# A macaron transformer step on one core: the opening with the first norm deferred for three panels, tile by tile

## The reference

```python
def modulation(cond, w_mod, b_mod):
    m = jax.nn.silu(cond) @ w_mod + b_mod
    return m.reshape(cond.shape[0], 1, N_MOD, D_MODEL)
def modulate(x, g, shift, scale):
    return rms_norm(x, g) * (1.0 + scale) + shift
def swiglu(h, w_in, w_out):
    g, u = jnp.split(h @ w_in, 2, axis=-1)
    return (jax.nn.silu(g) * u) @ w_out
...
    x = x + m[2] * (0.5 * swiglu(modulate(x, norm_g[0], m[0], m[1]), w_in[0], w_out[0]))
    out, aux = mixer(modulate(x, norm_g[1], m[3], m[4]))
    x = x + m[5] * out
    x = x + m[8] * (0.5 * swiglu(modulate(x, norm_g[2], m[6], m[7]), w_in[1], w_out[1]))
```

## Time and profile before

| | us |
|---|---|
| median of 3 runs | 1517.96 (1517.74 to 1518.47) |
| the profiled execution | 1518.2 |
| its span | 1515.8 |
| PE busy / weight loads busy | 1508.3 / 1446.7 |
| DVE busy | 1087.1 |
| ACT busy | 668.1 |

### The profile page before, as it was taken

How to read it: one execution, slowest core, us unless ns; L and a number is a source line. 1 busy time by engine, 2 the same in 40 slices (tenths; PEclk the granted TensorE clock), 3 DMA queues, 4 the chain that set the end, 5 groups by cost and what they waited for, 6 DMA issues and landing times.

```text
span 1515.8 us, 22012 instructions
## 1 busy us (share of the span) xinstructions
PE 1508.3 (100%) x8886; PEld 1446.7 (95%) x8886; DVE 1087.1 (72%) x1747; ACT 668.1 (44%) x1031; POOL 34.8 (2%) x45
## 2 busy tenths in 40 slices
PE   9999999999999999999999999999999999999999
PEld 5999999988889999999999999999997899999999
DVE  5887887789887887876678787877578876343332
ACT  5433333254686633333363333325458765333221
POOL 0000000000031000000000000000020000000000
PEclk9999999999999999999999999999999999999999
DMA  9756566543233365655455655654331033333233
GB/s 391 280 211 233 207 247 223 188 153 116 94 98 139 126 232 201 241 195 184 165 186 190 227 214 213 231 185 152 116 124 57 3 137 112 139 113 137 100 131 118
DMA packets 52276, 258.00 MB, mean 170 GB/s; under 512 B 6608, under 2 KB 8912, under 8 KB 37072
## 3 DMA queue, kind: packets, MB, share of 16 engines
q1 hardware_dynamic: 49632, 253.13, 46.2%
q10 hardware_dynamic: 2544, 3.48, 0.7%
HBM read 253.29 MB, written 3.29 MB: 169 GB/s over the span
## 4 chain that ended last, share of the span: by engine, by line
PE 96%; DVE 1%; DMA 1%; ACT 1%; issue 1%; SPq 0%; DVEq 0%; ACTq 0%
PE ps L2178 30%; PE ps L2180 29%; PE ps L2179 29%; PE ps L2830 1%; DMA wm_first<-in_w_mod_first 1%; PE ps L2721 1%; PE ps L2839 1%; PE ps L2853 1%; PE ps L2576 1%; PE ps L2545 1%; PE ps L2287 0%; PE ps L2505 0%; PE ps L2310 0%; PE ps L2563 0%; PE ps L2228 0%
## 5 line engine op out<-in xcount | busy, mean ns | idle before, releaser
L1375 DVE TENSOR_TENSOR w_lo<-w_raw,w_hi 128x2048 fp32r<-128x2048 f32 (+3 forms) x177 | 347.3, 1964 | 233.8 <-ACT w_hi L799 231.5
L2178 PE MATMUL ps<-hx_hi,w_hi 128*128 128x384 f32 (+1 forms) x1432 | 480.2, 335 | 0.0
L2179 PE MATMUL ps<-hx_lo,w_hi 128*128 128x384 f32 (+1 forms) x1432 | 478.6, 334 | 0.0
L2180 PE MATMUL ps<-hx_hi,w_lo 128*128 128x384 f32 (+1 forms) x1432 | 478.5, 334 | 0.0
L799 ACT ACTIVATE w_hi<-w_raw 128x2048 fp32r<-128x2048 f32 (+3 forms) x177 | 292.7, 1654 | 407.1 <-DMA w_raw<-in_w_out 210.7
L2178 PEld LDWEIGHTS ps<-hx_hi,w_hi 128*128 128x128 f32 x1432 | 268.9, 188 | 2.3 <-issue 1.8
L2179 PEld LDWEIGHTS ps<-hx_lo,w_hi 128*128 128x128 f32 x1432 | 268.9, 188 | 0.0
L2180 PEld LDWEIGHTS ps<-hx_hi,w_lo 128*128 128x128 f32 x1432 | 268.8, 188 | 0.0
L2180 PE MATMUL ps<-g_hi,w_lo 128*128 128x384 f32 x704 | 236.6, 336 | 0.0
L2178 PE MATMUL ps<-g_hi,w_hi 128*128 128x384 f32 x704 | 236.5, 336 | 0.0
L2179 PE MATMUL ps<-g_lo,w_hi 128*128 128x384 f32 x704 | 236.5, 336 | 0.0
(11 more groups left out here) (293 smaller groups left out, 1501.3 us busy)
## 6 DMA issues: line engine op xcount, KB each, us to landing
w_raw<-in_w_in SPq DMA_DIRECT2D x88, 1024.0 KB, 4.8
wm<-in_w_mod SPq DMA_DIRECT2D x128, 512.0 KB, 5.7
w_raw<-in_w_out SPq DMA_DIRECT2D x64, 704.0 KB, 4.1
w_raw<-in_w_qkv SPq DMA_DIRECT2D x12, 1024.0 KB, 4.8
wm_first<-in_w_mod_first SPq DMA_DIRECT2D x8, 1024.0 KB, 19.0
w_raw<-in_w_o SPq DMA_DIRECT2D x7, 1024.0 KB, 4.8
w_raw<-in_w_qup SPq DMA_DIRECT2D x8, 576.0 KB, 3.7
w_raw<-in_w_down SPq DMA_DIRECT2D x6, 704.0 KB, 4.0
```

The costliest lines, as they stand in the source:

```text
L1375: nc.vector.tensor_tensor(w_lo[:, slot, 0:width], w_raw[:, slot, 0:width], w_hi[:, slot, 0:width].bitcast(F32), ALU.subtract).then_inc(w_l ...
L2178: nc.tensor.matmul(out, l_hi, r_hi, start=first, stop=False)
L2179: nc.tensor.matmul(out, l_hi, r_lo, start=False, stop=False)
L2180: return nc.tensor.matmul(out, l_lo, r_hi, start=False, stop=last)
```

## The change

The first norm is deferred for three panels together. PE starts on `xg` of k = 0 as soon as its own gain is there, and takes panels 0, 1 and 2 k tile by k tile. Only k = 0 stays plain (`RAW = 1`, from the new tile `xg_raw`). The root is computed later, beside k = 3; the normed tiles, which from panel 3 on are used, are made beside k = 5 to 7 and overwrite `hx_hi`, `hx_lo`, where `xg` stood. The three panels come in quarters of 512 columns each (two k tiles of all three panels), so the layout of `w_in` in memory is k by k. Panel 3 is loaded without waiting into the last two slots of `wm`; the rows of `w_mod` wait for that. ACT rounds panel 4, and does SiLU and rounding for panels 0 to 2, still inside `first_norm`; the seven parameter DMAs come behind that, since one of them lands in a tile that the norm now uses, and the SiLU of `cond` comes after panel 5 is rounded. `mod_units` moves the modulation products of panels 0 to 2 to later ones.

```diff
-        return {0: 3, 1: 3 if m > 2 else 0, 2: 3 if m > 2 else 0, 3: 0}[f]
+        return {0: (2 if m < 5 else 4 if m > 9 and m % 2 == 0 else 3) if m > 2 else 0, 1: 3 if m > 2 else 0, 2: 3 if m > 2 else 0, 3: 0}[f]
...
-        DEFER = {2: 0, 3: 1, 5: 2}
+        DEFER = {0: 0, 2: 1, 3: 2, 5: 3}
...
+            if n == SLOTS:
+                return wm[:, WM_SLOTS - 2 + half, :]
...
+            load_first(0)
+            load_x(slice(0, 2), first_in[0])
+            load_quarter(0)
+            load_first(1)
+            load_first(2)
+            load_x(slice(2, 4), first_in[1])
+            load_quarter(1)
+            load_first(3)
+            load_x(slice(4, KD), x_in)
+            load_first(4)
+            load_quarter(2)
...
+            load(3, "in", 0, 3)
...
+                    if n == SLOTS + 1:
+                        sp.wait_ge(w_lo_done, SLOTS + 1)
...
             first_norm()
-            act.wait_ge(cond_in, 16)
-            nc.scalar.activation(cond[:], cond[:], ACT.Silu).then_inc(cond_ready, 1)
+            act.wait_ge(h_lo_done, h_val(0, KD - 1))
             for dst, name in ((ropes, "ropes"), (gq, "gq"), (gm, "gm"), (gmT, "gmT"), (subg, "subg"), (gdown, "gdown"),
                               (lamp, "lamp")):
                 act.dma_start(dst[:] if name != "lamp" else dst, d[name]).then_inc(params_in, 16)
-            ffn_in(0)
+            ffn_in(0, 3)
...
-                    zeros(9)
+                    zeros(3)
...
+                    mod_rows(0)
+                    mod_columns(0)
+                    zeros(2)
+                    plain(0, 0, 0)
...
+                    tiles(0, 5)
+                    mod_rows(7)
+                    tiles(1, 5)
+                    mod_columns(7)
+                    tiles(2, 5)
+                    for k in (6, 7):
+                        tiles(0, k)
+                    for k in (6, 7):
+                        for m in (1, 2):
+                            tiles(m, k)
```

More of the change, by code:

```diff
@@ L122, in build_step @@
         hx_hi = sb("hx_hi", [P, KD, TX], F32R)
+        with ExitStack() as part:
+            xg_raw = sb("xg_raw", [P, RAW, TX], where=part)
         with ExitStack() as part:
@@ L983, in ffn_in @@
                         high(base + m + 2)
+                    if f == 0 and m == start:
+                        act.wait_ge(cond_in, 16)
+                        nc.scalar.activation(cond[:], cond[:], ACT.Silu).then_inc(cond_ready, 1)
                     act.wait_ge(panel_used, base + m + 1)
@@ L1524, in norm @@
+                h_low(0, 7)
+                scale_out(0, 0, 1)
+                low(4)
+                first_panels(0)
+                scale_out(0, 0, 2)
+                gate(0, 2)
+                gate_low(0, 2)
             def norm(n, layer, part):
@@ L2331, in zeros, with tiles @@
                             nc.tensor.matmul(ps[:, 4, 0:T], hn[:, 0, 0:P], hn[:, 0, :], start=True, stop=True)
[L2333 to L2334 removed]
+                    pe.wait_ge(dve_consts, 1)
+                    def tiles(m, k):
+                        for half in range(2):
+                            tile(m, k, half)
+                    zeros(3)
                     pe.wait_ge(condT_ready, 1)
[L2336 removed]
+                    pe.wait_ge(dve_consts, 4)
@@ L2337, in ffn_in @@
                     mod_rows(0)
+                    mod_columns(0)
+                    zeros(2)
+                    plain(0, 0, 0)
+                    plain(0, 0, 1)
+                    plain(1, 0, 0)
+                    mod_rows(1)
+                    plain(1, 0, 1)
+                    plain(2, 0, 0)
+                    mod_columns(1)
+                    plain(2, 0, 1)
+                    mod_rows(2)
+                    tiles(0, 1)
+                    mod_columns(2)
+                    tiles(1, 1)
@@ L2338, in ffn_in @@
+                    tile(2, 1, 0)
+                    mod_rows(3)
+                    tile(2, 1, 1)
+                    tiles(0, 2)
+                    mod_columns(3)
+                    tiles(1, 2)
+                    mod_rows(4)
+                    tiles(2, 2)
+                    mod_columns(4)
+                    tiles(0, 3)
+                    pe.wait_ge(gains, 9)
                     sum_squares(0)
-                    mod_columns(0)
-                    zeros(1)
+                    tiles(1, 3)
```

462 lines of the change are left out of this document (275 added, 187 removed).

## The result

| | kernel before | changed kernel |
|---|---|---|
| median of the runs, us | 1518.22 (1517.74 to 1518.91, 6 runs) | 1527.99 (1524.97 to 1528.48, 6 runs) |
| ratio to before, 95% interval | | 1.0059 [1.0047, 1.0072] |
| profiled execution, span | 1515.8 | 1526.5 (its time 1528.48) |
| PE starts panel 3 / panel 5, us | 53.33 / about 70.0 | 55.48 / 78.29 |

A forecast was written before the change was run, and what follows sets the result against it. PE, busy for practically the whole span, was taken as the bound. Panel 3 starting 0.3 us later plus a 4.1 us wait at panel 5 made 4.4 on 1518.2; forecast 1522.5 us, range 1519.3 to 1525.0.

The forecast's parts named there:

- When PE can start: Opening: first plain product at 10.4, after the first wm_first piece at 6.7, further loads to 9.4 and xg of k = 0.
- Work to panel 3: PE's work from 10.4 to panel 3: 39.2 us in all, so a dense PE begins panel 3 at 49.6.
- the two extra columns: Tiles ahead of panel 3: two added columns cost 0.5% of the tiles, 0.1 us.
- Waits on the way: PE's waits before panel 3: 0.65 at k = 1, 1.1 and 2.1 at k = 7, 0.2 for scale_out; 4.0 us.
- The chains of ten steps: ACT and DVE chains to k = 7's columns and xg: summed to 4.8 and 4.7 us, PE waiting 1.1 and 2.1.
- Panel 4: Load to low part takes 8.96 us: no wait but no slack; a load slower by 0.5 would show as 0.3.
- Panel 5: Seven parameter DMA issues, 3.2 us, stand ahead of ACT's rounding of panel 5; PE waits 4.1 us.
- Rival 1: ACT's DMA issues before panel 5 fall in its idle time; PE waits only 1.2: 1519.7 us, chance 0.12.
- The clock: TensorE's clock behind its waits: nothing in the sum; a slower start, 2.0 us, stood only as a rival, chance 0.09.
- rival 4: Slow TensorE at the plain products or after the wait ahead of panel 5: one more start costs 2.0, 1524.6; chance 0.09.

The follow-up runs named there:

- Both fillers: Changed kernel with six extra fp32 products ahead of panel 5's waits and two between panel 0's k tiles 6 and 7: 1523.02 us, ratio 1.0033.

## Why the forecast was wrong in size

- **When PE can start**: right. First plain product at 10.52, forecast 10.4.
- **Work to panel 3**: 39.2 forecast. From 10.52 to 55.48 less the waits of 3.57 it is 41.4. Of the 2.2 between them 1.6 is the low-clock stretch. Another 0.4 is a mis-sized term: the two extra columns. I took 0.5% of the tiles. Products of 386 columns start 0.177 apart, products of 384 columns 0.173 apart, and 126 of them make 0.5, not 0.1.
- **Waits on the way**: 4.0 forecast, 3.57 measured, and each at its place: 0.65 against 0.54, 1.1 against 0.74, 2.1 against 1.94, 0.2 against none, and 0.35 for `wm_first` that I didn't have. The chains of ten steps came out 0.2 to 0.4 short of their sum.
- **Panel 4**: no wait forecast, 1.16 measured. The step said that there was no slack and gave the price of a slower load. The load was slower, 6.15 from issue to rounding where the earlier trace rows has 4.72; with 4.72 its low part would have been there at 63.6, just before PE was through with panel 3 at 64.0. The step called the queue of the earlier trace rows empty, and it wasn't (a `w_mod` load 0.37 behind), and it took one row where the kernel before has loads of 4.7 to 5.2. Why this load took 6.15 stays open. In two other profiles with the low-clock stretch ahead of it panel 4 waited only 0.21 and 0.37.
- **Panel 5**: right. 4.1 forecast, 4.55 measured; the issues took 3.64 from 70.26 to 73.90 instead of 3.2. That they start when the rounding of panel 2's product is let go was forecast, and they did (70.25, 70.26). Rival 1, the hidden issues, was wrong for this order, and the edit that puts the issues behind the rounding shows where it is right. (The rule of the Trainium skill, Perfetto Trace Analysis, section DVE / Act Engine Instruction, that the sequencer is free once an operation is in the wait queue, agrees with the issues beside the rounding at 69.75; it doesn't agree with the issue at 70.26, which held until the rounding ahead of it had its data. The measurement decides.)
- **The clock**: this is the step that failed. The sum of the forecast priced the waits of TensorE (4.0 in the opening, 4.1 at panel 5) at their length alone and the clock behind them at nothing. I had rival 4 at 2.0 us for one start at the lower level, at 0.09, as a thing apart from the forecast. It is no rival: it is a consequence of the forecast's own waits. Both fillers together give back 5.0 us: 1528.0 to 1523.0, nearly the 1522.5 of the forecast. (In the profiled execution the two low-clock stretches are 1.6 and 2.5; the load of panel 4 goes out 1.6 later for the first of them, and there panel 4 waits 1.2.) The price of a wait of 4.1 should have been 4.1 plus such a start, with most of the chance. (The Trainium skill, TensorE: Matmul & The Clock Gate, Part 1, has the array throttled again after it has idled. The traces agree in that every fall to 0.50 stands at or behind a wait of TensorE; but after the same wait of 1.94 one execution fell and one stayed at 1.00.) One caution on rival 4's own row: the granted clock of the kernel before reads 1.00 through the fillers too (0 to 8 us), so the lower level there was read from the spacing of the products alone.

## What to carry to other kernels

A wait of TensorE can cost twice, once as the wait and once as the low-clock stretch that may follow (here 1.6 us after 1.94 in one execution and nothing in another, and 2.5 after 4.55). The low-clock stretch also delays whatever waits for TensorE, loads above all. Here the DMA issues on ACT's queue cost nothing behind the instruction that was late, and some 0.5 us each ahead of it; their place in the list is worth as much as their existence. When a load is sized by a row, look at several of its kind: here they spread from 4.7 to 5.2, and the one that mattered took 6.15.

## What the runs showed of the hardware

- The granted clock fell to 0.50 after TensorE had been idle for 1.94 us, some 1.1 us after it had taken up work again (49.7), in the profiled execution of the changed kernel. With the issues behind the rounding it fell at about 48.5, right at the end of such a wait (1.95), and with the `w_mod` loads behind the load of panel 5 it didn't fall at all (1.94). After the waits of 4.17 to 4.86 us it fell in each profile. In the changed kernel it was back at 1.00 at 53.0 and at 83.6, with TensorE at work since 48.54 and 78.29. After the waits of 0.15 to 1.25 us of the opening and of panels 3 to 5, and after one of 1.86, it stayed at 1.00 in every profile.
- ACT's DMA issues start ahead of operations that stand before them in the list and have their data (issues at 69.44 to 72.83, while the rounding from 69.75 and the SiLU had been ahead of them), but not ahead of one that waits for data (70.25, 70.26).
- A panel load of 1 MB took 4.7 to 5.2 us to land with one or two `w_mod` loads 0.4 us behind it. With five of them 2.7 to 3.2 us behind it, it took 5.22 to 6.15 to its rounding, in one execution each of four kernels; whether they are the reason is not shown.
